# Gate products of a decoder layer's last stage: one token slice at a time, or three side by side

## The reference

```
mixed = sigmoid(g_a) * (o_attn @ w_br_attn) + sigmoid(g_s) * (o_ssm @ w_br_ssm)
x = x + mods[2] * (mixed @ w_out)
h = rms_norm(x, g_norm_mlp) * (1 + mods[4]) + mods[3]
x = x + mods[5] * (square(relu(h @ w_ff1)) @ w_ff2)
y = rms_norm(x, g_final)
```

## Time and profile before

| | |
|---|---|
| runs | median 2170.97 us of 3 (2167.47 to 2175.76) |
| profiled execution | 2170.92 us, of which its span is 2169.1 us |
| mean granted TensorE clock | 0.965 of full |
| busy in the span | PE 95%, PEld 85%, DVE 42%, ACT 35%, POOL 26% |
| last stage | from about 995 us to the end |
| gates of the last stage | 1003.5 to 1286.2 us |

### The profile page before, as it was taken

The page is one execution under the profiler, slowest core; times in us unless marked ns, Lnnn a source line. Parts: engine busy times, 40 slices in busy tenths (PEclk is TensorE's granted clock), DMA queues, the critical chain, the costliest instruction groups (busy, mean ns, idle before and its releaser), DMA issues.

```text
span 2169.1 us, 33731 instructions
## 1 busy us (share of the span) xinstructions
PE 2050.0 (95%) x13952; PEld 1839.7 (85%) x13952; DVE 904.8 (42%) x1743; ACT 769.8 (35%) x1572; POOL 568.6 (26%) x453
## 2 busy tenths in 40 slices
PE   6998999899899999787999999999999999999997
PEld 4765699788666677566999999999999999999997
DVE  5674321455566676464111134453134224313414
ACT  5131411445466777354222233332023113202303
POOL 0550000455234444331221221121221212212120
PEclk8989999999889999898999999999999999999999
DMA  9305134465123222875111131111111111111122
GB/s 359 97 1 143 25 79 113 162 233 198 59 65 79 64 79 64 326 301 202 49 40 50 49 118 40 40 40 49 49 40 49 49 40 49 46 43 49 40 59 81
DMA packets 207504, 201.54 MB, mean 93 GB/s; under 512 B 34134, under 2 KB 187710, under 8 KB 199080
## 3 DMA queue, kind: packets, MB, share of 16 engines
q1 hardware_dynamic: 194982, 131.40, 20.9%
q0 software_dynamic: 9792, 67.11, 8.2%
q10 hardware_dynamic: 2578, 0.88, 0.2%
HBM read 177.62 MB, written 21.58 MB: 92 GB/s over the span
## 4 chain that ended last, share of the span: by engine, by line
PE 52%; DMA 1%; DVE 0%; ACT 0%; SPq 0%; issue 0%; ACTq 0%; DVEq 0%
PE ps L2333 17%; PE ps L2331 17%; PE ps L2332 17%; PE ps L2477 1%; DMA tail<-x_keep 1%; DMA tail<-in_w_in 1%; PE ps L2498 0%; DVE tail L2842 0%; ACT tail L2671 0%; DVE tail L2818 0%; SPq L2443 0%; SPq L2456 0%; ACT tail L2662 0%; DVE tail L2760 0%; ACT tail L2576 0%
## 5 line engine op out<-in xcount | busy, mean ns | idle before, releaser
L2331 PE MATMUL ps<-tail,tail 128*128 128x356 f32 (+2 forms) x2304 | 756.5, 328 | 9.8 <-POOL tail L2729 9.4
L2333 PE MATMUL ps<-tail,tail 128*128 128x356 f32 (+2 forms) x2304 | 750.1, 326 | 0.0
L2332 PE MATMUL ps<-tail,tail 128*128 128x356 f32 (+2 forms) x2304 | 748.2, 325 | 0.0
L2729 POOL TENSOR_TENSOR tail<-tail,tail 128x1024 fp32r<-128x1024 f32 x96 | 232.5, 2421 | 926.4 <-ACT tail L2576 926.4
L2331 PEld LDWEIGHTS ps<-tail,tail 128*128 128x128 f32 x2304 | 435.2, 189 | 12.9 <-POOL tail L2729 9.6
L2332 PEld LDWEIGHTS ps<-tail,tail 128*128 128x128 f32 x2304 | 435.4, 189 | 2.6 <-issue 0.2
L2333 PEld LDWEIGHTS ps<-tail,tail 128*128 128x128 f32 x2304 | 435.5, 189 | 0.0
L2576 ACT ACTIVATE tail<-tail 128x1024 fp32r<-128x1024 f32 x96 | 101.0, 1052 | 320.8 <-PE ps L2333 314.3
L2760 DVE SCALAR_TENSOR_TENSOR tail<-ps,mod,tail 128x346 f32<-128x346 f32 (+2 forms) x120 | 68.7, 573 | 346.4 <-PE ps L2333 336.3
L1734 POOL TENSOR_SCALAR pr<-pr,row_reciprocals,gT 128x640 f32<-128x640 f32 (+7 forms) x128 | 99.3, 786 | 145.2 <-DVE row_reciprocals L1860 142.6
L2631 ACT ACTIVATE tail<-tail,tail 128x346 f32<-128x346 f32 (+2 forms) x96 | 56.0, 583 | 195.6 <-DVE tail L2800 100.2
(11 more groups left out here) (510 smaller groups left out, 2975.0 us busy)
## 6 DMA issues: line engine op xcount, KB each, us to landing
tail<-in_w_ff SPq DMA_DIRECT2D x64, 512.0 KB, 3.8
wada_late<-in_w_ada SPq DMA_DIRECT2D x32, 512.0 KB, 4.2
wada<-in_w_ada SPq DMA_DIRECT2D x4, 2048.0 KB, 11.7
tail<-in_w_in SPq DMA_DIRECT2D x16, 512.0 KB, 3.6
x_keep<-xT SPq DMA_DIRECT2D x1, 4224.0 KB, 23.7
h_keep<-hT SPq DMA_DIRECT2D x1, 4224.0 KB, 13.7
tail<-x_keep SPq DMA_DIRECT2D x1, 4224.0 KB, 13.8
xrow<-in_x_prompt SPq DMA_DIRECT2D x8, 512.0 KB, 8.0
```

Source lines behind the costliest of these rows:

```text
L2331: pe.matmul(out, whi[:, kw, :], xlo(kx), start=(i == 0), stop=False)
L2332: pe.matmul(out, wlo[:, kw, :], xhi(kx), start=False, stop=False)
L2333: mm = pe.matmul(out, whi[:, kw, :], xhi(kx), start=False, stop=(i == n - 1))
L2729: pool.tensor_tensor(wlo[:, x % 2], wraw[:, x % 2], whi[:, x % 2], ALU.subtract).then_inc(w_split, 1)
```

## The change

For j = 1 and j = 2 the loop over slices moves inside. The three results n, n + 1, n + 2 of a tile are built up together in three banks: for each block k of the contraction and each of the three kinds of product, the three slices follow one another with the same stationary weights, and each goes to its own bank. The three results are finished by the last three matmuls of the tile. j = 0 stays as it was, and so does everything outside this loop: the number of matmuls, their shapes, and the other engines' programs.

The waits move as well. All three slices now stand behind one wait at the tile's start: `h_split` at 3 for the first gate tile, and `kept` at n - 5 in place of n - 7 before each result.

```
             for x in range(OUT0):
                 f, j = x // 3, x % 3
                 pe.wait_ge(w_split, x + 1)
-                for s in range(3):
-                    if j == 0:
+                if j == 0:
+                    for s in range(3):
                         for i, (_, hi, lo) in enumerate(sources):
...
-                    else:
-                        n = 12 * f + 3 + 3 * j + s
-                        if f == 0 and j == 1:
-                            pe.wait_ge(h_split, s + 1)
-                        if n >= 8:
-                            pe.wait_ge(kept, n - 7)
-                        gemm(bank[n % 8][:, 0:width(s)], x, hhi, hlo, tok(s), every).then_inc(products, 1)
+                else:
+                    n = 12 * f + 3 + 3 * j
+                    if f == 0 and j == 1:
+                        pe.wait_ge(h_split, 3)
+                    if n + 2 >= 8:
+                        pe.wait_ge(kept, n - 5)
+                    for k in range(KD):
+                        for i, (w, v) in enumerate(((whi, hlo), (wlo, hhi), (whi, hhi))):
+                            for s in range(3):
+                                mm = pe.matmul(bank[(n + s) % 8][:, 0:width(s)], w[:, x % 2, k, :], v[:, k, tok(s)],
+                                               start=k == 0 and i == 0, stop=k == KD - 1 and i == 2)
+                                if k == KD - 1 and i == 2:
+                                    mm.then_inc(products, 1)
```

## The result

| | before | changed |
|---|---|---|
| executions | 4, median 2170.01 us (2167.47 to 2175.76) | 4, median 2190.79 us (2182.16, 2185.49, 2196.09, 2198.67) |
| profiled execution | 2170.92 us, span 2169.1 | 2182.16 us, span 2180.4 |
| mean granted clock | 0.965 | 0.963 in the profiled one; 0.962, 0.956, 0.956 in the others |

The ratio is 1.0084 with a 95% interval of 1.0045 to 1.0123: slower, and outside the range of 2167 to 2188 us on record. The profiled execution is 11.2 us longer than the one before; the forecast for it was 8.7.

What follows compares the result with a forecast made beforehand. The stage was taken to be paced by PE, busy 95% of the span. Terms 6.06 + 1.8 + 0 + 0.8 + 0 = +8.7 us on 2170.92 gave 2179.6 us, with an 8 in 10 range of 2167 to 2188.

Steps and rivals of the forecast that it cites:

- the sums of the bounds: Whole kernel: the terms' lower bounds add to -3.4 us and the upper to +14.4; the 8 in 10 range includes them.
- Start of the first gate tile: Before the first gate tile PE waits for slice 2 of h's low part instead of slice 0: +6.06 us.
- The clock after it: After PE's 6.4 us idle before the first gate tile the clock runs lower: +1.8 us, bounds 0 and 2.0.
- Middle tiles: Gate tiles between first and last: evictions and weight splits at each tile's end stay hidden under PE's work: 0 us.
- The matmuls themselves: The 1152 reordered gate matmuls: shared stationary weights and changed banks save nothing, 0 us, bounds -8 and +3.5.
- End of the gates: Last gate tiles to out product: it starts 4.4 us later, mostly covered by the x_keep stop; +0.8 us, bounds -1.5 and +2.8.
- The sum: Whole kernel: all terms together +8.7 us, 2179.6 us; the forecast itself had chance 0.60.
- shared weights pay: Reordered gate matmuls: one stationary tile for three removes the 15.5 ns excess, -17.9 us, total 2161.8 us; chance 0.08.
- loads set the pace: Reordered gate matmuls: weight loads of 0.188 us could not overlap as now, +30 us, about 2210 us; chance 0.07.
- the clock swings: Gate tiles: short stops between banks lower the clock for a third of reordered matmuls, +50 us, about 2230 us; chance 0.02.
- A second locked split: End of the gates: lock order goes against the change again, another 2.4 us split in the way, 2182.0 us; chance 0.10.
- the clock spare the first stop: First gate tile: 6.06 us wait without lowered clock, end of the gates fully covered, 2177 us; chance 0.13.

Runs made afterwards that it cites:

- a3: The kernel before with only the wait changed: the first gate tile waits for all three low parts of h; median 2176.2 us, ratio 1.0033.
- b1: The changed kernel with the last feature block's two gate tiles in the old order; ratio 1.0017 to the kernel before.
- b2: The changed kernel with each block's nine matmuls in diagonal order, neighbours mostly differing in stationary tile as well as bank; 35.01 us a feature block, ratio 1.0027.
- b4: The changed kernel with 36 extra matmuls in front of the first gate tile, into a bank it then overwrites; ratio 1.0025 to the kernel before.
- d4: The kernel before with slices of 352 columns and the out product's sums of squares one result later; median 2167.5 us, ratio 0.9937.
- d2: The changed kernel with three slices of 352 columns instead of 346, 356 and 354; median 2167.1 us, ratio 0.9976 to the kernel before.
- a4: The changed kernel with the first gate tile and the last feature block's two in the old order, 13 tiles in the new; median 2171.4 us, ratio 1.0005.
- c1: The kernel before with the three products of a block reordered so the stationary tile repeats in 24 of 72 matmuls; one execution, 2169.8 us.
- d1: The kernel before, in its old order, with slices of 352 columns; median 2161.5 us, ratio 0.9943.
- b3: The changed kernel with the two inner loops swapped, so the bank changes at each third matmul; 34.92 us a feature block, ratio 1.0024 to the kernel before.

## Why the prediction missed

**The range failed, at the step "takes in the sums of the bounds: 2167 to 2188".** The interval was built from the terms of one execution. The difference between executions stood in it at nothing, because the three runs shown agreed, and they had all fallen in one group by chance. The runs showed a second group, 14 to 15 us longer, for the kernel before and the changed one alike. An upper bound of +14.4 us on the work, with an execution 15 us longer behind it, would have reached some 2200. That both kernels have the longer executions was shown (batches a to d). The five traces of the lower group (a3, b1, b2, b4, d4) lose their time between 100 and 300 us, at a clock of 0.82 to 0.85 where the other traces have 0.87 to 0.92. None of the kernel before's long executions was traced; that they lose it in the same place is inferred from their mean clock. What tips an execution into one or the other was not tried.

**Start of the first gate tile, +6.06**: right. PE started 9.20 us after the first low part instead of 3.19, +6.01, released by L2848, in all traces of this wait.

**The clock after it, +1.8 within 0 and 2.0**: right in kind; measured 2.3 and 1.5 in the two traces of the changed kernel (272.74 and 272.00, less 268.77 and 1.7 for the order) and 1.66 with the wait alone. The upper bound was too low by 0.3. b4 shows that the stop is the cause. The way to the number, which placed 6.4 us between stops of 3.6 and 9.4, does not hold: the longest stop of these traces, 8.3 us (d2), cost the least, 1.4. Nor was a lower clock certain: the 3.4 to 3.6 us stop in the out product was followed by one in the kernel before, in a4, b1, c1 and d1, and not in a3. The Trainium skill, "TensorE: Matmul & The Clock Gate", says under Part 1: The HAM clock gate that the gate's watching runs free of what the kernel does, so that the turning point varies from run to run; the two outcomes after nearly the same stop fit that.

**Middle tiles, 0 for waits**: right; PE has no wait between 1024 and 1296 us.

**The matmuls themselves, 0 within -8 and +3.5**: the size was off, inside its bounds. It was 16 x 0.105 = +1.7 us. The reasoning from the 512-column pairs was right as far as it went: neither the repeated stationary tile (c1) nor the bank (b2) costs. What I left out was that 346, 356 and 354 are not 512 or 352: beside slices of 352 columns, uneven ones already cost the old order 0.45 us a block and the new one 0.67. My excess of 15.5 ns over the columns at 2.4 GHz was read as one thing, and 2 ns of it belonged to the widths. Why the order matters with uneven slices stays open: the changed order adds 0.22 us a block, b2's, which changes slice and bank as often, adds none, and b3's saves 0.09.

**End of the gates, +0.8 within -1.5 and +2.8**: right. 1.1 and 0.3 in the two traces. The meeting of POOL and DVE came at 1293.2, 8.7 us after ACT's first gate of the tile (1284.47), as worked out (8.8), the instruction held up by POOL took 4.94 us, and the stop of 3.6 us for x_keep took up the rest. Taking the clock's loss as the same was off: after the stop ahead of the out product the clock was 0.50 and then 0.85 over two stretches of 4 us in the changed kernel's trace (a loss of 2.6 us) and 0.61 and 0.96 in its repeat (1.7), against 1.4 in the kernel before. This makes the difference between 1.1 and 0.3.

**The sum** for the profiled execution was +8.7 and came out at +11.1 in the stage: 6.0 + 2.3 + 1.7 + 1.1. The like-with-like difference of executions is 10.6 to 11.4 us. In the repeat's trace it was 9.5. So the direction held, the likeliest case was 0.8 and 2.4 us too low in the two traces, and the like-with-like difference is just at the 0.5% that I had put between "the same" and "slower". The rivals that shared weights pay, that loads set the pace and that the clock swings were all wrong: 0.22 us a block leaves no room for them, and the clock was 1.00 from 1050 to 1296 us. A second locked split did not occur, nor did the clock spare the first stop.

## What to carry to other kernels

When results that used to be ready one by one are made ready together, look at both ends of the loop: the first wait becomes the latest of the inputs (6 us here), and all consumers start at once, where a lock or a long copy that was hidden behind a slice no longer is. What the reorder is meant to save should be seen in a trace first: here each matmul brought its own load of weights, and neighbours with the same weights ran no faster.

Take the spread from many executions before a range is given: three that agree within 0.4% said nothing of a second group 0.7% longer. To judge a change of this size, cut the traces at marks on both sides of it: the stage's own length differed by 1.5 us between two traces of the changed kernel, and the distance of two blocks by 0.01, where the executions differed by 20.

Choose slice widths before loop orders: going from 346/356/354 to 352/352/352 gave 10 us in a stage of 1155, more than any order.

## What the runs showed of the hardware

- A matmul of 352 columns with a split operand starts every 0.160 us; at 346, 356 and 354 columns the mean is 0.162 although the columns are as many. The old order lost 0.45 us in 216 matmuls, the changed one 0.67, and 348/356/352 in that order 0.16. Both the width and the starting column count: 24 matmuls of 356 columns took 3.95 us from column 346 on and 3.90 from column 348, and from column 0 on 346 columns took longer than 348 (3.85 against 3.82).
- Same stationary tile as the neighbour, another bank than the neighbour: neither changed the pace at 352 columns (34.56 us a block in both orders).
- POOL's split and a DVE subtraction of two operands did not run together: begun 0.09 us behind the split, the subtraction took 4.94 us instead of 2.75.
- A stop of 5.9 to 8.3 us cost another 1.4 to 2.3 us through the clock, and the longest not the most; matmuls without use in its place avoided that (b4).
- The same program ran at a mean granted clock of 0.962 to 0.967 in 60 of 98 executions and of 0.954 to 0.961 in 38. In the traces of long executions of its variants the loss lies between 100 and 300 us.
